# The head of a two-block layer kernel: inputs loaded first, a third of the modulation beside them, the rest in the memory scan

## What is computed

```python
mod_x = (silu(c) @ ada_w + ada_b)[:, None, :]          # 1024 -> 6 * 1024
mod_c = (silu(c_ctx) @ ada_w + ada_b)[None, None, :]
sh1x, sc1x, g1x, sh2x, sc2x, g2x = split(mod_x, 6)
zx = (rmsnorm(x, norm1_g) * (1 + sc1x) + sh1x) @ w_in
zc = (rmsnorm(ctx, norm1_g) * (1 + sc1c) + sh1c) @ w_in
... # gated linear scan and mLSTM scan over zc, zx, both directions
x = x + g1x * (mixer output @ w_out)
x = x + g2x * moe(rmsnorm(x, norm2_g) * (1 + sc2x) + sh2x)
```

## Time and profile before

| | us |
|---|---|
| median of 3 runs | 4635.69 |
| lowest and highest run | 4631.91, 4639.19 |
| the profiled execution's own time | 4640.43 |
| its span | 4638.7 |
| PE busy (share of the span) | 3951.1 (85%) |
| DVE busy | 2179.4 (47%) |
| ACT busy | 1524.1 (33%) |
| POOL busy | 1068.9 (23%) |

### The profile page before, as it was taken

One profiled execution on the slowest core, in us unless ns is written; L12 is line 12 of the kernel. 1 busy time (PEld: TensorE's weight loads), 2 busy tenths in 40 slices (PEclk: granted clock), 3 DMA queues, 4 the chain that ended last, 5 costly groups with the idle time before them and its releaser, 6 DMA issues. The chain is left out here.

```text
span 4638.7 us, 45964 instructions
## 1 busy us (share of the span) xinstructions
PE 3951.1 (85%) x17556; PEld 3078.1 (66%) x17556; DVE 2179.4 (47%) x2406; ACT 1524.1 (33%) x1900; POOL 1068.9 (23%) x570
## 2 busy tenths in 40 slices
PE   7499989837649999973598887999988899999998
PEld 1278878826537887851376664777766678888886
DVE  0357734451248888863554433222223564345335
ACT  0331211020237777752342122222222233233233
POOL 0122210012021111110233111222203334444443
PEclk9789977868569999985799788999988999999999
DMA  6221210033159999983143112111105433333323
GB/s 243 74 77 54 81 67 31 34 129 139 42 230 398 401 401 397 402 320 118 64 148 115 45 51 77 66 65 64 61 27 190 147 112 94 97 96 96 96 90 106
DMA packets 143843, 642.99 MB, mean 139 GB/s; under 512 B 18552, under 2 KB 33768, under 8 KB 127040
## 3 DMA queue, kind: packets, MB, share of 16 engines
q1 hardware_dynamic: 113600, 550.08, 32.5%
q10 hardware_dynamic: 20400, 61.35, 3.4%
q0 software_dynamic: 9680, 29.29, 1.7%
HBM read 537.05 MB, written 103.62 MB: 138 GB/s over the span
## 5 line engine op out<-in xcount | busy, mean ns | idle before, releaser
L2805 POOL TENSOR_TENSOR t_wl<-t_raw,t_wh 128x1024 fp32r<-128x1024 f32 (+1 forms) x176 | 398.2, 2265 | 544.1 <-ACT t_wh L2857 544.0
L99 PE MATMUL m_b<-b_high,m_high 128*128 128x512 f32 x960 | 414.0, 431 | 44.0 <-POOL m_low L131 44.0
L100 PE MATMUL m_b<-b_rest,m_high 128*128 128x512 f32 x960 | 393.2, 410 | 0.0
L101 PE MATMUL m_b<-b_high,m_low 128*128 128x512 f32 x960 | 384.1, 400 | 0.0
L129 POOL TENSOR_TENSOR m_high<-m_raw,m_one 128x1024 fp32r<-128x1024 f32 x60 | 121.1, 2018 | 871.4 <-PE m_b L101 817.9
L99 PE MATMUL t_b<-b_high,t_wh 128*128 128x512 f32 x768 | 302.8, 394 | 18.9 <-POOL t_wl L2805 18.8
L100 PE MATMUL t_b<-b_rest,t_wh 128*128 128x512 f32 x768 | 300.5, 391 | 0.0
L101 PE MATMUL t_b<-b_high,t_wl 128*128 128x512 f32 x768 | 300.3, 391 | 0.0
L2857 ACT ACTIVATE t_wh<-t_raw 128x1024 fp32r<-128x1024 f32 (+1 forms) x176 | 175.6, 999 | 336.2 <-PE t_b L101 287.6
L99 PE MATMUL zs_z<-zs_hs,zs_high 128*128 128x512 f32 (+1 forms) x632 | 243.6, 385 | 38.2 <-POOL zs_low L448 38.2
L99 PEld LDWEIGHTS m_b<-b_high,m_high 128*128 128x128 f32 x960 | 187.2, 195 | 106.3 <-POOL m_low L131 45.3
(11 more groups left out here) (619 smaller groups left out, 9100.7 us busy)
## 6 DMA issues: line engine op xcount, KB each, us to landing
ex_raw<-in_expert_w SPq DMA_DIRECT2D x118, 2048.0 KB, 10.3
t_raw<-in_w_ff SPq DMA_DIRECT2D x128, 512.0 KB, 3.5
m_raw<-in_w_ug SPq DMA_DIRECT2D x60, 512.0 KB, 4.4
ada_w<-in_ada_w SPq DMA_DIRECT2D x12, 2048.0 KB, 7.7
yrows<-ex_y ACTq DMA_DIRECT2D x38, 512.0 KB, 11.4
gates<-m_ob SPq DMA_DIRECT2D x32, 512.0 KB, 2.9
me_g<-gates SPq DMA_DIRECT2D x32, 512.0 KB, 3.7
zs_raw<-in_w_in_s SPq DMA_DIRECT2D x29, 512.0 KB, 3.6
```

Source lines behind the costliest of these rows:

```text
L99: nc.tensor.matmul(out, w[0], x[0], start=first, stop=False)
L100: nc.tensor.matmul(out, w[0], x[1], start=False, stop=False)
L101: return nc.tensor.matmul(out, w[1], x[0], start=False, stop=last)
L2805: self.nc.gpsimd.tensor_tensor(self.wl[u % self.NW][:, 0:m], self.raw[u % 2][:, 0:m], self.wh[u % self.NW][:, 0:m].bitcast(F32), ALU.subtr ...
```

## The change

- `modulation` and `first_norm` are gone as stages. A class `Head` does their work inside the stage of `first_scans`, without a barrier. SP issues three small loads, the context, x in two halves, and then the first 16 of 48 tiles of `ada_w` (128 x 1024, 512 KB each) through a ring of seven buffers; the first two projection tiles go ahead of the last two of these.
- The modulation matmul is turned round: the tile of `ada_w` is the weights (128 x 128) and `cs` moves, two columns wide, so that the results lie on the partitions at once. The transposes go.
- ACT squares each part of the input as it comes, DVE adds the squares up over the channel blocks, and PE makes one sum with the ones per part, ahead of tiles 3, 6 and 9.
- DVE scales x in place, then applies gain and shift; ACT makes the rounded copy; the subtraction is shared by DVE (even blocks) and POOL (odd blocks). The first projection pieces wait for their own part alone.
- The other 32 tiles of `ada_w` follow the 29 projection tiles through the same two buffers `raw`. PE multiplies them (one column: x alone) in the last four chunks of the memory scan, 3, 3 and 2 in the three fills. The twelve projection pieces go into the first four chunks of x, one per fill. DVE adds the bias at the end of the stage.
- The zeros of the clear are 128 wide, not 256, which makes the packets 512 bytes and twice as many.

```diff
+class Head:
+    NT, RING = 2 * KD, 7
+    PIECES = [(0, BANK), (BANK, BANK), (2 * BANK, CTX)]
+    def load(self, sp, between):
+        sp.dma_start(self.cs[:], self.A["c2"]).then_inc(self.c_in, 16)
+        sp.dma_start(self.bias[:], self.A["ada_b"]).then_inc(self.c_in, 16)
+        sp.dma_start(self.gain[:, 0, :], self.A["norm1_g"]).then_inc(self.c_in, 16)
+        sp.dma_start(self.x[:, :, 0:CTX], self.A["ctxT"]).then_inc(self.x_in[0], 16)
+        for c in range(2):
+            sp.dma_start(self.x[:, :, CTX + c * BANK:CTX + (c + 1) * BANK], self.A["xT"][:, :, c * BANK:(c + 1) * BANK]).then_inc(self.x_in[1 + c], 16)
+        for n in range(self.NT):
+            if n >= self.RING:
+                sp.wait_ge(self.used, n - self.RING + 1)
+            if n == self.NT - 2:
+                between()
+            sp.dma_start(self.w[n % self.RING][:], self.A["ada_w"][n]).then_inc(self.w_in[n % self.RING], 16)
...
+    def tensor(self, pe):
+        for n in range(self.NT):
+            if n in (3, 6, 9):
+                i = n // 3 - 1
+                a, m = self.ARRIVALS[i]
+                pe.wait_ge(self.gathered, (KD - 1) * (i + 1))
+                mm_(self.ps[i][:, 0:m], self.C["ones"][:], self.acc[:, a:a + m], start=True, stop=True).then_inc(self.summed, 1)
+            pe.wait_ge(self.w_in[n % self.RING], 16 * (n // self.RING + 1))
+            for k in range(KD):
+                mm = mm_(self.pm[:, 2 * n:2 * n + 2], self.w[n % self.RING][:, k * P:(k + 1) * P], self.cs[:, k, :], start=k == 0, stop=k == KD - 1)
+            mm.then_inc(self.used, 1)
...
+    def vector(self, dve):
...
+        for i, (a, m) in enumerate(self.ARRIVALS):
+            dve.wait_ge(self.rooted, i + 1)
+            V.reciprocal(self.rs[:, a:a + m], self.rs[:, a:a + m]).then_inc(self.inverted, 1)
+            dve.wait_ge(self.inverted, i + 1)
+            for k in range(KD):
+                V.tensor_tensor(self.x[:, k, a:a + m], self.x[:, k, a:a + m], self.rs[:, a:a + m], ALU.mult).then_inc(self.scaled, 1)
...
 class Inputs:
     def load(self, sp, n):
-        if n >= 2:
+        if n >= N_Z + 2:
+            sp.wait_ge(self.modulated, n - N_Z - 1)
+        elif n >= 2:
             sp.wait_ge(self.split[n % 2], n // 2)
...
+    def modulate(self, pe, count):
+        for i in range(self.rest, min(self.rest + count, N_REST)):
+            n = N_Z + i
+            if i == 0:
+                pe.wait_ge(self.taken, len(self.pieces) - len(self.banks) + 1)
+            pe.wait_ge(self.w_in[n % 2], 16 * (n // 2 + 1))
+            for k in range(KD):
+                mm = self.nc.tensor.matmul(self.banks[len(self.pieces) % len(self.banks)][:, i:i + 1], self.raw[n % 2][:, k * P:(k + 1) * P], self.head.cs[:, k, 0:1],
+                                           start=k == 0, stop=k == KD - 1)
+            mm.then_inc(self.modulated, 1)
...
-MEMORY_FILLS = [(0, 0, 0)] * 2 + [(1, 0, 0), (1, 1, 0)] * 4
+MEMORY_FILLS = [(0, 0, 0)] * 2 + [(1, 1, 1)] * 4 + [(0, 0, 0)] * 4
+MODULATION_FILLS = [(0, 0, 0)] * 6 + [(3, 3, 2)] * 4
...
-        blank = s.sb("blank", [P, CTX])
+        blank = s.sb("blank", [P, P])
```

More of the change, by code:

```diff
@@ L319, in _ @@
                 dve.wait_ge(left, KD)
[L323 to L361, removed]
-                for n in range(nt):
-                    mm = nc.tensor.transpose(pt[:, 2 * n:2 * n + 2], rows[:, n * P:(n + 1) * P], C["ident"][0:2, 0:2])
-                mm.then_inc(turned, 1)
-            @block.vector
-            def _(dve):
-                with dve.Fori(0, slabs_ // 3) as i:
-                    for j in range(3):
-                        dve.wait_ge(used[j], i + 1)
-                        nc.vector.tensor_copy(rows[:, bass.ds((i * 3 + j) * BANK, BANK)], ps[j][0:2, :]).then_inc(taken[j], 1)
-                dve.wait_ge(c_in, 32)
-                dve.wait_ge(turned, 1)
-                st = Steps(dve, own)
-                st.then(nc.vector.tensor_tensor(mod[:], pt[:, 0:2 * nt].rearrange("p (n s) -> p n s", s=2),
-                                                bias[:].unsqueeze(2).broadcast_to([P, nt, 2]), ALU.add))
@@ L462, in multiply, with bias @@
             self.made += 1
+    def modulate(self, pe, count):
+        for i in range(self.rest, min(self.rest + count, N_REST)):
+            n = N_Z + i
+            if i == 0:
+                pe.wait_ge(self.taken, len(self.pieces) - len(self.banks) + 1)
+            pe.wait_ge(self.w_in[n % 2], 16 * (n // 2 + 1))
+            for k in range(KD):
+                mm = self.nc.tensor.matmul(self.banks[len(self.pieces) % len(self.banks)][:, i:i + 1], self.raw[n % 2][:, k * P:(k + 1) * P], self.head.cs[:, k, 0:1],
+                                           start=k == 0, stop=k == KD - 1)
+            mm.then_inc(self.modulated, 1)
+            self.rest += 1
+    def bias(self, dve):
+        dve.wait_ge(self.modulated, N_REST)
+        self.nc.vector.tensor_tensor(self.head.mod[:, Head.NT:, 0], self.banks[len(self.pieces) % len(self.banks)][:, 0:N_REST], self.head.bias[:, Head.NT:], ALU.add).then_inc(self.biased, 1)
+        dve.wait_ge(self.biased, 1)
     def arrived(self, eng, i):
@@ L1032, in _, with first @@
             def _(sp):
-                Z.load(sp, 0)
-                Z.load(sp, 1)
+                def first():
+                    Z.load(sp, 0)
+                    Z.load(sp, 1)
+                head.load(sp, first)
                 lin.load(sp)
                 for n in range(N_Z):
-                    if n + 2 < N_Z:
-                        Z.load(sp, n + 2)
+                    Z.load(sp, n + 2)
                     if n == 0:
@@ L1048, in _ @@
                         Z.store(sp, n)
+                for n in range(N_Z + 2, N_Z + N_REST):
+                    Z.load(sp, n)
                 for j in range(3):
@@ L1056, in _ @@
                 nc.gpsimd.memset(blank[:], 0.0).then_inc(C["blanked"], 1)
-                Z.halve(pool)
+                Z.fill(pool)
+                Z.halve(pool, range(2))
+                head.gpsimd(pool)
+                Z.halve(pool, range(2, N_Z))
             @block.tensor
             def _(pe):
+                head.tensor(pe)
                 Z.multiply(pe, 4)
```

153 lines of the change are left out of this document (115 added, 38 removed).

## The result

| | before | after |
|---|---|---|
| median of 8 runs each, us | 4635.31 | 4648.84 |
| lowest and highest | 4631.91, 4639.19 | 4645.20, 4655.07 |
| the profiled execution's own time | 4640.43 | 4648.82 |
| its span | 4638.7 | 4646.8 |

The ratio is 1.0031, 95% interval 1.0020 to 1.0042: slower by 13.5 us, a little more than the 9 us that can be told from no change. The profiled executions lie 8.4 us apart, since that of before stands 5 us above its median and that of after at its own.

What follows compares the result with a forecast made beforehand. PE was taken to bound the memory scan. Terms -107.8 + 1.5 + 3 + 103.8 = +0.5 us gave 4640.9 on the profiled execution, which stands 4.7 above the median, so 4636 us; bounds 4623 to 4649.

Steps and rivals of the forecast that it cites:

- The head: Start to first projection matmul: 93 us instead of 200.80, PE's tiles ending at 81.8 and VectorE's chain at 80.1; gain 107.8.
- falls between 54 and 66 us and is covered too: In the head: GpSimd's halving of the first two projection tiles, four operations of at most 2.5 us, costs nothing.
- The stall before the second piece: Projections after the head: PE stalls up to 3 us while the second and third pieces are split; taken as 1.5.
- The clear of yrows: 8 MB clear in 512-byte packets lands between 26.6 us and twice that, ahead of projection tile 5's load; cost nothing.
- Three-piece chunks: First four chunks of x in the memory scan: six more pieces, +33, less gaps, waits and low-clock time; +3 in all.
- Modulation chunks: Last four memory-scan chunks: scan work 30.5, tiles 27.4, load waits 1.4, so 59.3 each; 232 against 128.2, loss 103.8.
- pays eight weight loads instead: Each of the 48 modulation tiles loads eight 128x128 weights instead of streaming 512 columns; 3.43 us at low clock, 1.72 at high.
- in every stretch that has narrow work alone: PE's clock throughout: 1.2 GHz, not 2.4, expected wherever only narrow matmuls run.
- The clock stays up: Rival: gapless narrow matmuls keep 2.4 GHz in head and scan, 4524 us, or only in the scan, 4542; chance 0.09.
- Loads land late: Rival: in the scan's fills a tile's load takes 7.7 us, adding 31 us, 4667 us; chance 0.11.
- Tiles vanish in waits: Rival: another engine bounds the scan, so tiles fit in PE's waits and nearly the whole head is gained, 4532; chance 0.02.
- a clock of 0.5: Sign of being right: tiles of about 3.4 us at this granted clock both in the head and in the scan.

Runs made afterwards that it cites:

- experiment 5: The changed kernel with the first two projection tiles' loads issued behind modulation tile 6 instead of 13: 4647.5 us, one run.
- experiment 6: The changed kernel with all 24 subtractions of the split on VectorE, none on GpSimd: 4639.4 us, one run.
- Experiment 2: The changed kernel with one repeated projection piece (24 wide matmuls, result unused) added in each of the four last chunks: 4623.1 us, one run.
- experiment 1: The changed kernel without the 32 modulation tiles beside the memory scan and their loads: 4414.5 us, total not comparable; last four chunks 109 us for 229.

## Why the prediction was right or wrong

The forecast was 4636 us in the frame of the median; 4648.8 came, 13 us more and at the upper edge of its bounds (4649). "No change" had been given 0.48 and "slower" 0.24, and slower came. For the profiled execution it was 4640.9 against 4648.8. The mechanism was right: as much as the head gains is paid back in the last four chunks, in tiles of 3.43 us at 0.50. The sum was short by 8 us (profiled): head +7.5, way to the scan +4.4, first four chunks -1.6, last four -3.0, and 0.6 outside these terms. It was luck that two of the misses went the other way: without them the sum would have been short by 12.5.

- **The head, -107.8: the largest miss, 7.5.** It gave -100.25. DVE's chain ended at 86.8, where PE at 81.8 had been taken as the last. Of that, DVE's start on the third mean is 3.5 us late (61.35 for 57.8: 1.4 from the landing of the first weight tile, the rest because a sum of 512 columns takes PE 1.9 us and that of 256 1.0, in all 4.7 and not 2.3), and its chain is 25.5 us instead of 22.3. Then the split takes 12.9 and not 10. The failing steps are the price of the three sums, and that scalings and split were taken at rows without POOL beside them: without POOL there the first projection matmul comes 1.8 us earlier (experiment 5) or 2.4 (experiment 6), and PE's own tiles end at 85.0, 3.2 behind the forecast. The prediction said of the halving on GpSimd that it "falls between 54 and 66 us and is covered too", and asked only for its time, not for what it does to its neighbour: 4.0 us in the scalings (experiment 5). In the split POOL's help made a pair 3.12 us where DVE alone needs 2.50 (experiment 6). The Trainium skill (SBUF — State Buffer, Who interferes with whom) says that DVE and GpSimd share a pair of ports under an exclusive lock, and that who issues second is blocked for the whole of the other's instruction. The rows agree on the blocking: DVE's operation of 89.69 ends at 91.18, POOL's of 89.77 at 91.03. By the records it was the earlier one that waited, but the starts are 0.08 us apart and spans on POOL are rough, so this does not settle who issued first.
- **The stall before the second piece, +1.5: wrong.** The way from the first projection matmul to the scan is 5.9 us longer, 4.4 more than the term. The wait is 4.0, the one for the gates 1.1 longer, and 0.8 is in the matmuls themselves: without PE's waits the way took 461.8 us before and 462.6 after. In experiment 6 it took 459.1 without its waits. The number of wide matmuls at the low pace goes with that: 48 before, 50 after, 32 in experiment 6, each 0.2 us longer. So the kernel before had paid as much for low clock on this way. The wait itself comes, as in the split, from POOL beside DVE: it is gone in experiment 6.
- **The clear of yrows, 0: right.** It landed after 28.7 us (26.6 before) and tile 5 was in time.
- **Three-piece chunks, +3: right**, +1.4, with the opening blocks at the full clock behind the third piece.
- **Modulation chunks, 59.3 each and 232 in all, +103.8: right**, 58.4, 229.2 and +100.8 with the 2.1 us that come back. Tiles 27.8 a chunk (27.4), waits for loads 4.3 us in the four, 2.5 of them one wait in the first (5.6), the rest the scan's own work at the low clock. The loads landed in 3.6 us, where the sum had 3.6 to 4.3. The estimate of 3.2 us from the Trainium skill (DMA: Bandwidth & Descriptors, Anatomy of one DMA) is 0.4 below the trace.
- **The explanation of these chunks: right in direction, too simple.** The prediction gave 64 us to the tiles and the rest to the clock that the scan's own work loses. Experiment 2 shows the clock's part by bringing 50 us back with useless work. The tiles' own time is half clock as well: 3.43 us at 0.50, 1.8 at 1.00, as the prediction had it (1.72). Its sentence that each tile "pays eight weight loads instead" does not give the loss; streamed at 0.54 a load takes 3.38 us. And experiment 1 shows that narrow work alone is not always at 1.2 GHz: "in every stretch that has narrow work alone" holds in the head, by its pace, and in all tiles of the scan but the first two, but not in the later half of two of the four empty chunks.
- **The rivals.** The clock stays up: no, 0.50 in all tiles of the scan but the first two. Loads land late: no, 3.6 us. Tiles vanish in waits: no, PE is 99% busy. The last rival's ground, that DVE's 57 of 128 us speak against it, was used in the experiments the other way round: DVE had room for the work that PE had not.

## What to carry to other kernels

For a matrix times one or two vectors, held or streamed, 512 KB took PE 1.7 to 1.9 us at 2.4 GHz and 3.4 at 1.2 GHz. In these runs the streamed form (512 moving columns) mostly kept the high clock and the held form (one or two moving columns) did not. So stream such a matrix, or give it to VectorE with its accumulating form (1.22 us). Work that moves "beside" a loop is beside it only if the loop's bounding engine is not the one that does it; and narrow work put where wide work stood can leave its neighbours at the low clock as well. Before pricing an operation on VectorE or GpSimd at its row, ask whether the other one runs at the same time, and before adding a load to a queue, ask what the entry ahead of it waits for.

## What the runs showed of the hardware that was not expected

- Adding 96 wide matmuls made the program 26 us faster (one run), since the granted clock rose from 0.50 to 0.99 for what stood behind them.
- A tile held as weights takes 1.8 us at a clock of 1.00 and 3.43 at 0.50; a streamed load of the same size takes 1.8 to 1.9 at 1.00 and 3.38 at 0.54.
- A wait of PE of 4.0 us was followed by 13 wide matmuls at the low pace (111.8 to 117.3 us), though the work behind it was wide from its first matmul on.
- The granted clock rose to 1.00 twice among the scan's own matmuls of 128 columns and fewer (experiment 1, at 803 and about 827 us), the first time after some 60 us of the same work at 0.50. What decides it is open.
- The page's clock column shows 1.00 for the head's tiles, though their pace, 3.43 us a tile from 26 to 85 us, is the one that they have at 0.50 in the scan. The pace of a known instruction is the better witness there; the prediction's signs asked for "a clock of 0.5" in the head, which the column does not show.
- DVE's operations of 0.41 and 0.35 us take 1.49 and, over eight, 0.85 when GpSimd works beside them; a pair of blocks with six operations on DVE alone (2.50 us) was faster than one with five on DVE and one on GpSimd (3.12).
